# One recurrence block in float32: matrix powers turned by VectorE's 32x32 block transpose instead of by products of transposes, and the grams of two pairs of heads formed beside the powers of two others

## The chip, the cores and the metric

The kernel runs on one core of one Trainium2 chip. The metric is device microseconds of that core. The kernel before took 3894.08 us, the median of three runs (3888.68, 3894.08 and 3894.92 us).

## The reference, cut to what matters

The program is four phases: two transformer layers with different mixers (A and B), a third block with windowed attention (C) and a mixture of experts (D). The change touches only the recurrence in phase B, the RWKV-7 mixer: 16 heads of 64 channels, 512 time steps.

```python
def step(state, inp):
    r_t, w_t, k_t, v_t, a_t, b_t = inp
    sa = jnp.einsum('bhij,bhj->bhi', state, a_t)
    state = (state * w_t[:, :, None, :] + sa[..., None] * b_t[:, :, None, :]
             + v_t[..., None] * k_t[:, :, None, :])
    y_t = jnp.einsum('bhij,bhj->bhi', state, r_t)
    return state, y_t
_, ys = lax.scan(step, state0, seq_inputs)
```

The kernel does it by chunks of 32 steps. With the decays folded into the operands, the steps inside a chunk hang together by a strictly triangular 32x32 matrix N for each head (the masked products of the b and a rows), and the kernel needs the inverse of 1 - N, which is the product (1 + N)(1 + N^2)(1 + N^4)(1 + N^8)(1 + N^16). Four chunks stand on the diagonal of one 128x128 matrix.

## The kernel before, in words

Time is cut into four tiles of 128 steps (`tl` = 0 to 3), heads into eight pairs (`q` = 0 to 7, two heads `u` each). For each tile TensorE does four stages in this order (L2521 to L2545): the *rows* stage turns three operands so that time lies on partitions (24 transposes, each bank of four copied out by ScalarE, L2236); the *pair* stage makes the inverse and what follows from it for all eight pairs; the *chunk* stage runs the state through four chunks one after the other; the *y* stage forms the outputs (L2447, L2451), which VectorE adds to the rest (L2485).

The pair stage goes by groups of two pairs, so there are four groups for each tile and 16 in all. Each engine has its own list of steps (`PAIR_PE`, `PAIR_DVE`, `PAIR_ACT`), and in a group each step is done for one pair and then for the other. Nothing of a group starts before the group ahead has ended: the two pairs of a group fill all four banks of `BK`, and `pp_gram` waits until the last copies of the pairs two before it (`w1_ready`, `w2_ready`) are out. The steps of a pair are:

- *grams*: eight products of 64-row operands (L2286), which VectorE masks out of PSUM (L2355, L2362); ScalarE copies the part that the y stage needs (L2247);
- *low*: the transposed N is had from two more products (L2294), masked by VectorE (L2372), beside 1 + N (L2370);
- *level 1*: N times N (L2313), the transposed square (L2323), and two products with the value rows (L2319, L2321), which VectorE copies out (L2378, L2380);
- *levels 2 to 4*: the next power (L2313, not at level 4), the product of the transposed power with the running inverse (L2315) and the next transposed power (L2323). ScalarE copies both powers out (L2259, L2262) and VectorE adds the product to the running inverse (L2392);
- *last*: the product with the sixteenth power (L2333), added by VectorE;
- *end*: the inverse is put to use in two products for each head (L2343, L2344), copied out by VectorE (L2401) and ScalarE (L2268).

All of it is float32, and one 128x128x128 product appears as two MATMUL records. Where N and its transpose are both wanted, TensorE makes each by a product of its own.

## Time and profile before

| what | us |
|---|---|
| median of three runs | 3894.08 |
| the profiled execution | 3894.22 |
| its span | 3892.4 |
| TensorE matmul busy in the span | 3422.6 (88%) |
| VectorE busy | 1117.3 (29%) |
| ScalarE busy | 1068.5 (27%) |
| mean granted TensorE clock | 0.919 of full |

The recurrence takes the span from about 1122 to 1668 us. A share of busy time says how long an engine had an instruction in flight, not how fast it went; the granted clock is 1.00 at 2.4 GHz and 0.50 at 1.2 GHz. A timeline row gives start, length, engine, line and operation; in square brackets stands how long the engine had been idle and what it had waited for. An instruction's length contains its way through the engine, so that the distance between two starts on a full engine is shorter than the length.

### The profile page before, as it was taken

What the parts mean: (1) busy time and instruction counts of PE and PEld (TensorE: products, weight loads), DVE (VectorE), ACT (ScalarE), POOL (GpSimd) and SP (SyncE); (2) the same over time, 40 slices, a digit from 0 to 9 for tenths busy, and PEclk for the clock granted to TensorE, in tenths of its full rate; (3) what the DMA queues carried; (4) which work ended last, traced back from release to release, by engine and by line L of the source; (5) the groups of instructions that cost most, each with busy time, mean ns of one, the idle gap of its engine ahead of it and who ended that gap; (6) DMA issues with size and microseconds to landing.
All of it is one profiled execution on the core that took longest, in us unless ns stands there. A gap on an engine that the chain in (4) does not pass through costs nothing.

```text
span 3892.4 us, 39687 instructions
## 1 busy us (share of the span) xinstructions
PE 3422.6 (88%) x16652; PEld 2352.5 (60%) x16652; DVE 1117.3 (29%) x1836; ACT 1068.5 (27%) x1818; POOL 709.3 (18%) x344
## 2 busy tenths in 40 slices
PE   7998899979758898888889999988899986989896
PEld 5675688856447777756568876455685562333332
DVE  5342310142763433353231122275131220000001
ACT  3542433334331211213243332134321121111111
POOL 3021344422200000002134441000241121000000
PEclk9999999988877977889999999999999988999998
DMA  3231244311100000022122323210122237989996
GB/s 112 87 108 44 87 162 134 99 58 52 49 0 2 1 1 1 12 87 81 44 82 92 98 87 99 76 33 1 49 77 79 81 119 303 387 327 372 375 375 279
DMA packets 217759, 448.62 MB, mean 115 GB/s; under 512 B 14192, under 2 KB 191376, under 8 KB 204656
## 3 DMA queue, kind: packets, MB, share of 16 engines
q1 hardware_dynamic: 200832, 400.58, 28.4%
q10 hardware_dynamic: 6720, 25.17, 1.6%
q0 software_dynamic: 10032, 20.35, 1.5%
q8 instruction: 133, 2.18, 0.2%
q14 instruction: 42, 0.34, 0.0%
HBM read 502.67 MB, written 31.46 MB: 137 GB/s over the span
## 4 chain that ended last, share of the span: by engine, by line
PE 77%; DMA 8%; DVE 7%; ACT 4%; issue 3%; POOL 1%; SPq 0%; ACTq 0%; POOLq 0%; DVEq 0%
PE product_banks L560 12%; PE product_banks L561 12%; PE product_banks L562 12%; PE product_banks L532 8%; PE product_banks L1859 5%; PE product_banks L1892 3%; DMA A<-in_w_up 3%; DMA Wr<-expert_rows 3%; PE product_banks L624 3%; PE product_banks L2323 2%; PE product_banks L2313 1%; PE product_banks L2315 1%; PE product_banks L1122 1%; PE score_banks L1103 1%; PE product_banks L1339 1%
## 5 line engine op out<-in xcount | busy, mean ns | idle before, releaser
L469 POOL TENSOR_TENSOR Wr_parts<-Wr,Wr_parts 128x1024 fp32r<-128x1024 f32 x186 | 447.2, 2406 | 1429.8 <-ACT Wr_parts L446 1429.8
L561 PE MATMUL product_banks<-A_parts,Wr_parts 128*128 128x512 f32 x1408 | 559.1, 397 | 0.0
L446 ACT ACTIVATE Wr_parts<-Wr 128x1024 fp32r<-128x1024 f32 x186 | 196.0, 1058 | 729.9 <-PE product_banks L562 636.1
L1859 PE MATMUL product_banks<-A,Wr 128*64 128x512 f32 x1504 | 338.9, 598 | 15.7 <-DMA A<-in_w_up 13.3
L560 PE MATMUL product_banks<-H_parts,Wr_parts 128*128 128x512 f32 x728 | 297.2, 408 | 24.4 <-POOL Wr_parts L469 20.8
L561 PEld LDWEIGHTS product_banks<-A_parts,Wr_parts 128*128 128x128 f32 x1408 | 269.6, 191 | 62.0 <-issue 2.2
L560 PE MATMUL product_banks<-A_parts,Wr_parts 128*128 128x512 f32 x680 | 269.8, 397 | 31.1 <-DVE A_parts L482 15.6
L562 PE MATMUL product_banks<-H_parts,Wr_parts 128*128 128x512 f32 x728 | 290.9, 400 | 0.0
L469 POOL TENSOR_TENSOR shared_con_parts<-Wr,shared_con_parts 128x1024 fp32r<-128x1024 f32 x80 | 193.1, 2414 | 446.5 <-ACT shared_con_parts L446 446.5
L562 PE MATMUL product_banks<-A_parts,Wr_parts 128*128 128x512 f32 x680 | 267.8, 394 | 0.0
L1859 PEld LDWEIGHTS product_banks<-A,Wr 128*64 128x64 f32 x1504 | 112.4, 138 | 237.4 <-issue 234.4
L561 PE MATMUL product_banks<-A_parts,shared_con_parts 128*128 128x512 f32 x600 | 239.8, 400 | 0.0
L1892 PE MATMUL product_banks<-A,Wr 128*64 128x512 f32 x752 | 180.9, 627 | 26.7 <-ACT Wr L1928 26.7
L1955 DVE TENSOR_TENSOR Wr<-product_banks,Wr 128x512 f32<-128x512 f32 x24 | 16.6, 692 | 606.9 <-PE product_banks L1859 606.9
L560 PEld LDWEIGHTS product_banks<-H_parts,Wr_parts 128*128 128x128 f32 x728 | 139.4, 192 | 63.5 <-POOL Wr_parts L469 25.8
L560 PEld LDWEIGHTS product_banks<-A_parts,Wr_parts 128*128 128x128 f32 x680 | 129.9, 191 | 63.3 <-POOL Wr_parts L469 18.7
L446 ACT ACTIVATE shared_con_parts<-Wr 128x1024 fp32r<-128x1024 f32 x80 | 84.7, 1059 | 300.5 <-PE product_banks L562 267.4
L2060 DVE SCALAR_TENSOR_TENSOR A<-product_banks,SC 128x512 f32<-128x512 f32 x64 | 44.0, 691 | 415.2 <-PE product_banks L562 415.1
L562 PEld LDWEIGHTS product_banks<-H_parts,Wr_parts 128*128 128x128 f32 x728 | 139.3, 191 | 33.4
L532 PE MATMUL product_banks<-A,Wr 128*128 128x512 f32 (+2 forms) x432 | 148.5, 504 | 0.0
L532 PE MATMUL product_banks<-H,Wr 128*128 128x512 f32 (+1 forms) x384 | 142.1, 531 | 6.5 <-issue 6.5
L562 PEld LDWEIGHTS product_banks<-A_parts,Wr_parts 128*128 128x128 f32 x680 | 129.7, 191 | 27.6
(430 smaller groups left out, 5459.0 us busy)
## 6 DMA issues: line engine op xcount, KB each, us to landing
A<-in_w_gate SPq DMA_DIRECT2D x32, 2048.0 KB
A<-in_w_up SPq DMA_DIRECT2D x32, 2048.0 KB
A<-in_w_down SPq DMA_DIRECT2D x32, 2048.0 KB
Wr<-in_m_w_up SPq DMA_DIRECT2D x32, 1024.0 KB, 5.3
Wr<-in_m_w_down SPq DMA_DIRECT2D x32, 1024.0 KB, 4.9
Wr<-in_w_in SPq DMA_DIRECT2D x32, 1024.0 KB, 5.6
Wr<-in_c_w_kv SPq DMA_DIRECT2D x16, 1024.0 KB, 5.2
expert_rows<-LB ACTq DMA_DIRECT2D x12, 1024.0 KB, 4.2
```

The costliest lines, as they stand in the source:

```text
L446: nc.scalar.activation(weight_parts(s)[0], loaded_part(s), ACT.Copy).then_inc(*mark("weights_high", s))
L469: nc.gpsimd.tensor_tensor(lo, loaded_part(s), hi, ALU.subtract).then_inc(*mark("weights_split", s))
L532: mm = pe.matmul(bank[0:m, 0:width], w[:, k, j * P:j * P + m], rhs(kk), start=(kk == 0), stop=(kk == L.kt - 1))
L560: pe.matmul(bank[:, :], hi[:, k, :], x_hi, start=(kk == 0), stop=False)
L561: pe.matmul(bank[:, :], hi[:, k, :], x_lo, start=False, stop=False)
L562: mm = pe.matmul(bank[:, :], lo[:, k, :], x_hi, start=False, stop=(kk == L.kt - 1))
L624: mm = pe.matmul(bank[:, 0:ww], lhs(k, m), w[:, k, :], start=(k == 0), stop=(k == L.kc - 1))
L1103: mm = pe.matmul(scores[:, q, :], tile(16 + h * dt + d)[:, q * P:(q + 1) * P], key_tile(tag, h * dt + d), start=(d == 0), stop=(d == dt - 1))
L1859: mm = pe.matmul(BK[r, 0 if kind == "gate" else 1, :], XT[b % 2][:, k * P + CAP * h:k * P + CAP * h + CAP], unit_rows((kind, b, h))[:, k, ...
L1892: mm = pe.matmul(BK[r, 2 + n, :], HT[b % 2][:, k * P + CAP * h:k * P + CAP * h + CAP], unit_rows(("down", b, h))[:, k, n * T:(n + 1) * T], ...
L2060: nc.vector.scalar_tensor_tensor(out=tile(40 + j % 4), in0=ps[:, :], scalar=0.0, in1=RS[:, :], op0=ALU.max, op1=ALU.mult).then_inc(*mark(" ...
L2323: mm = pe.matmul(bank[:, 0, 256 + u * P:256 + (u + 1) * P], N, A_, start=True, stop=True)
```

## The change

The transposed powers are no longer made by products. TensorE forms only the next power (`square_pe`) and the product with the running inverse (`inverse_pe`). ScalarE copies the power out, and VectorE turns it with `nc.vector.transpose`, which turns each 32x32 block by itself; as N and its powers are zero outside the 32x32 blocks on the diagonal, that is the whole transpose. The *low* products, their mask and the constant for it are gone.

The banks are shared out anew: `BK` holds only grams; powers and outputs of a pair take half a bank each (`turn_bank` and `stat_bank`); the inverse's products take the `score_banks`, and so does the y stage. Powers, running inverses and turned powers have buffers of their own for two successive groups, and each mask or addition now covers both heads of a pair in one instruction of 128x256 (or 128x512). `lmask` is gone from the constants, the outputs' mask writes its target directly (no copy by ScalarE), and the copies of the value products and of `W2` move from VectorE to ScalarE, whose list follows TensorE's order: powers of level 1, outputs of the two pairs before, value products, powers of levels 2 to 4.

The order of the pair stage is new. The grams of the next two pairs stand behind the first square of the current two, and the *end* of the two pairs before stands behind these. The grams of a tile's first two pairs are formed ahead: for tile 0 before the rows stage, for the others between the chunk stage and the y stage of the tile before. The rows stage moves into a function of its own and is otherwise the same. Lines of the new functions, and of the loops around them:

```diff
@@ -2239,170 +2256,204 @@
+        def square_bank(q):
+            return heads2((B6, B7)[q % 2][:, 0:256])
+        def out_bank(q):
+            return (B6, B7)[q % 2][:, 256:512]
+        def inverse_bank(q):
+            return heads2(S2[:, q % 2, 0:256])
+        def power_act(act, tl, q, level):
+            act.wait_ge(*at("square_done", (tl, q, level)))
+            if level == 1:
+                act.wait_ge(*at("inverse_started", (tl, q)))
+            nc.scalar.activation(power(q), square_bank(q), ACT.Copy).then_inc(
+                *mark("power_ready", (tl, q, level)))
+        def av_act(act, tl, q):
+            act.wait_ge(*at("av_done", (tl, q)))
+            nc.scalar.activation(tile(Y0 + q)[:, tl * P:(tl + 1) * P], out_bank(q)[:, 0:128],
+                                 ACT.Copy)
+            nc.scalar.activation(AV[q % 2], heads2(out_bank(q)[:, 128:256]), ACT.Copy).then_inc(
+                *mark("av_ready", (tl, q)))
+        def pair_out_rows_act(act, tl, q):
             act.wait_ge(*at("pair_done", (tl, q)))
+            nc.scalar.activation(W2[:, :, q, :], heads2(out_bank(q)[:, 0:128]), ACT.Copy)
+            nc.scalar.activation(W1T[:, q, :], out_bank(q)[:, 128:256], ACT.Copy).then_inc(
                 *mark("w1_ready", (tl, q)))
...
+        def gram_pe(pe, tl, q):
             if q >= 2:
-                pe.wait_ge(*at("w2_ready", (tl, q - 2)))
-                pe.wait_ge(*at("w1_ready", (tl, q - 2)))
+                pe.wait_ge(*at("rb_kept", (tl, q - 2)))
             elif tl:
-                pe.wait_ge(*at("wkv_added", (tl - 1, 1)))
+                pe.wait_ge(*at("rb_kept", (tl - 1, q + 6)))
...
+        def square_pe(pe, tl, q, level):
+            pe.wait_ge(*at("power_turned", (tl, q, level - 1)))
+            if level == 2:
+                pe.wait_ge(*at("av_ready", (tl, q)))
             for u in range(2):
+                mm = pe.matmul(square_bank(q)[:, u, :], turned_power(q, level - 1)[:, u, :],
+                               power(q)[:, u, :], start=True, stop=True)
+            mm.then_inc(*mark("square_done", (tl, q, level)))
+        def inverse_pe(pe, tl, q, level):
+            pe.wait_ge(*at("power_turned", (tl, q, level - 1)))
+            if level > 2:
+                pe.wait_ge(*at("inverse_ready", (tl, q, level - 1)))
+            else:
+                pe.wait_ge(*at("inverse_started", (tl, q)))
+                if tl and q < 2:
+                    pe.wait_ge(*at("wkv_added", (tl - 1, 1)))
             for u in range(2):
+                mm = pe.matmul(inverse_bank(q)[:, u, :], turned_power(q, level - 1)[:, u, :],
+                               inverse(q)[:, u, :], start=True, stop=True)
+            mm.then_inc(*mark("inverse_product_done", (tl, q, level)))
+        def av_pe(pe, tl, q):
+            pe.wait_ge(*at("grams_masked", (tl, q)))
+            pe.wait_ge(*at("power_ready", (tl, q, 1)))
+            if q >= 2:
+                pe.wait_ge(*at("w1_ready", (tl, q - 2)))
             for u in range(2):
                 h = 2 * q + u
+                v = VR[:, tl, h * 64:(h + 1) * 64]
+                pe.matmul(out_bank(q)[:, 128 + 64 * u:192 + 64 * u], GM[q % 2][:, u, 0:128], v,
+                          start=True, stop=True)
+                mm = pe.matmul(out_bank(q)[64 * u:64 * u + 64, 0:128], v,
+                               GM[q % 2][:, u, 128:256], start=True, stop=True)
+            mm.then_inc(*mark("av_done", (tl, q)))
+        def pair_end_pe(pe, tl, q):
+            pe.wait_ge(*at("inverse_ready", (tl, q, 5)))
+            if q < 6:
+                pe.wait_ge(*at("power_ready", (tl, q + 2, 1)))
+            for u in range(2):
+                h = 2 * q + u
+                X_ = inverse(q)[:, u, :]
+                pe.matmul(out_bank(q)[:, u * 64:u * 64 + 64], X_, AV[q % 2][:, u, :],
+                          start=True, stop=True)
+                mm = pe.matmul(out_bank(q)[64 * u:64 * u + 64, 128:256],
                                ROW[:, 0, h * 64:(h + 1) * 64], X_, start=True, stop=True)
             mm.then_inc(*mark("pair_done", (tl, q)))
+        def pairs_pe(pe, tl):
+            for q0 in range(0, 8, 2):
+                two = (q0, q0 + 1)
+                for q in two:
+                    square_pe(pe, tl, q, 1)
+                for q in two if q0 < 6 else ():
+                    gram_pe(pe, tl, q + 2)
+                for q in two if q0 else ():
+                    pair_end_pe(pe, tl, q - 2)
+                for q in two:
+                    av_pe(pe, tl, q)
+                for level in (2, 3, 4):
+                    for q in two:
+                        square_pe(pe, tl, q, level)
+                    for q in two:
+                        inverse_pe(pe, tl, q, level)
+                for q in two:
+                    inverse_pe(pe, tl, q, 5)
+            for q in (6, 7):
+                pair_end_pe(pe, tl, q)
+        def strict_dve(dve, tl, q):
             dve.wait_ge(*at("grams_done", (tl, q)))
+            nc.vector.tensor_tensor(power(q), gram_banks(q)[:, :, 0:128], gmask(0), ALU.mult).then_inc(
+                *mark("strict_ready", (tl, q)))
+        def turn_dve(dve, tl, q, level):
+            dve.wait_ge(*(at("power_ready", (tl, q, level)) if level else at("strict_ready", (tl, q))))
+            nc.vector.transpose(turned_power(q, level), power(q)).then_inc(
+                *mark("power_turned", (tl, q, level)))
+        def inverse_start_dve(dve, tl, q):
+            dve.wait_ge(*at("strict_ready", (tl, q)))
+            if q >= 4:
+                dve.wait_ge(*at("pair_done", (tl, q - 4)))
+            nc.vector.tensor_tensor(inverse(q), power(q), ident[:, None, :].broadcast_to([P, 2, P]),
+                                    ALU.add).then_inc(*mark("inverse_started", (tl, q)))
+        def keys_masked_dve(dve, tl, q):
+            dve.wait_ge(*at("grams_done", (tl, q)))
+            if q >= 2:
+                dve.wait_ge(*at("av_done", (tl, q - 2)))
+            nc.vector.tensor_tensor(GM[q % 2], gram_banks(q)[:, :, 256:512], gmask(2, 2),
+                                    ALU.mult).then_inc(*mark("grams_masked", (tl, q)))
+        def outputs_masked_dve(dve, tl, q):
+            if tl and q < 2:
+                dve.wait_ge(*at("wkv_done", (tl - 1, 1)))
+            nc.vector.tensor_tensor(RB[:, 2 * q:2 * q + 2, :], gram_banks(q)[:, :, 128:256], gmask(1),
+                                    ALU.mult).then_inc(*mark("rb_kept", (tl, q)))
+        def inverse_dve(dve, tl, q, level):
+            dve.wait_ge(*at("inverse_product_done", (tl, q, level)))
+            if level == 2:
+                dve.wait_ge(*at("inverse_started", (tl, q)))
+            else:
+                dve.wait_ge(*at("inverse_ready", (tl, q, level - 1)))
+            nc.vector.tensor_tensor(inverse(q), inverse_bank(q), inverse(q), ALU.add).then_inc(
+                *mark("inverse_ready", (tl, q, level)))
+        def pair_begin_dve(dve, tl, two):
+            for q in two:
+                strict_dve(dve, tl, q)
+            for q in two:
+                turn_dve(dve, tl, q, 0)
+            for q in two:
+                inverse_start_dve(dve, tl, q)
+        def pairs_dve(dve, tl):
+            for q0 in range(0, 8, 2):
+                two, ahead = (q0, q0 + 1), q0 < 6
+                for q in two:
+                    turn_dve(dve, tl, q, 1)
+                if ahead:
+                    pair_begin_dve(dve, tl, (q0 + 2, q0 + 3))
+                for level in (2, 3, 4):
+                    for q in two:
+                        turn_dve(dve, tl, q, level)
+                    for q in two:
+                        inverse_dve(dve, tl, q, level)
+                    if ahead and level < 4:
+                        keys_masked_dve(dve, tl, q0 + level)
+                    elif ahead:
+                        outputs_masked_dve(dve, tl, q0 + 2)
+                for q in two:
+                    inverse_dve(dve, tl, q, 5)
+                if ahead:
+                    outputs_masked_dve(dve, tl, q0 + 3)
...
@@ -2438,9 +2489,10 @@
         def y_pe(pe, tl):
 
             pe.wait_ge(*at("rb_kept", (tl, 7)))
-            pe.wait_ge(*at("w2_ready", (tl, 7)))
+            pe.wait_ge(*at("u_ready", 4 * tl + 3))
+
             def out_of(q, u):
-                return BK[64 * u:64 * u + 64, 2 * u + q // 4, (q % 4) * P:(q % 4 + 1) * P]
+                return S2[64 * u:64 * u + 64, q // 4, (q % 4) * P:(q % 4 + 1) * P]
 
             for q in range(8):
                 for u in range(2):
...
+            pe.wait_ge(*at("tilde_ready", 7))
+            for q in (0, 1):
+                gram_pe(pe, 0, q)
             for tl in range(TT):
...
+                rows_pe(pe, tl)
                 pe.wait_ge(*at("rows_ready", (tl, 2, 1)))
-                pe.wait_ge(*at("rows_ready", ("v", TT - 1, 1)))
-                for q0 in range(0, 8, 2):
-                    for f in PAIR_PE:
-                        for q in (q0, q0 + 1):
-                            f(pe, tl, q)
+                pairs_pe(pe, tl)
                 for c in range(4):
                     chunk_pe(pe, tl, c)
                     if tl == TT - 1:
                         norm_sum(pe, "a1_m", 2 * c, 2 * c + 1, width=M)
+                if tl < TT - 1:
+                    for q in (0, 1):
+                        gram_pe(pe, tl + 1, q)
                 y_pe(pe, tl)
             gn_pe(pe)
             product(pe, "w_o", parts(0, 8), low_ready("y"))
...
             nc.vector.memset(ST[:, 0, :, :], 0.0).then_inc(*mark("state_ready", 0))
+            pair_begin_dve(dve, 0, (0, 1))
+            for q in (0, 1):
+                keys_masked_dve(dve, 0, q)
+            for q in (0, 1):
+                outputs_masked_dve(dve, 0, q)
             for tl in range(TT):
-                for q0 in range(0, 8, 2):
-                    for f in PAIR_DVE:
-                        for q in (q0, q0 + 1):
-                            f(dve, tl, q)
+                pairs_dve(dve, tl)
                 for c in range(4):
                     chunk_dve(dve, tl, c)
                 if tl == TT - 1:
                     memory_norm(dve, "a1_")
+                else:
+                    pair_begin_dve(dve, tl + 1, (0, 1))
+                    for q in (0, 1):
+                        keys_masked_dve(dve, tl + 1, q)
                 y_dve(dve, tl)
+                if tl < TT - 1:
+                    for q in (0, 1):
+                        outputs_masked_dve(dve, tl + 1, q)
             gn_dve(dve)
```

## Rows read from the trace of the kernel before

**Rows 1.** The page's busy times and granted clock by slices (whole span).

```profile
PE 3422.6 (88%) x16652; PEld 2352.5 (60%) x16652; DVE 1117.3 (29%) x1836; ACT 1068.5 (27%) x1818; POOL 709.3 (18%) x344
...
PEclk9999999988877977889999999999999988999998
```

**Rows 2.** Pair stages by stretches: us, PE/PEld/DVE/ACT/POOL busy, clock, DMA share, GB/s.

```profile
1127.56:1222.41 94.85, 86.78 (x640) 73.75 (x640) 37.18 (x120) 24.43 (x72) 0.00 (x0) 0.87 0.00 1
1265.04:1354.05 89.01, 80.94 (x642) 69.48 (x644) 37.18 (x120) 24.43 (x72) 0.00 (x0) 0.94 0.00 1
1397.60:1491.10 93.50, 85.40 (x641) 73.11 (x641) 37.18 (x120) 24.43 (x72) 0.00 (x0) 0.89 0.00 1
1533.60:1627.10 93.50, 85.43 (x642) 73.17 (x642) 37.18 (x120) 24.44 (x72) 0.08 (x1) 0.89 0.00 1
```

**Rows 3.** Busy time by stretches: tile 0's y stage, tile 1's rows stage.

```profile
1246.50:1259.40 12.90, 12.90 (x162) 9.78 (x160) 1.38 (x2) 0.00 (x0) 0.00 (x0) 0.50 0.01 3
1259.40:1265.00 5.60, 4.65 (x28) 3.63 (x26) 2.58 (x4) 3.37 (x6) 0.00 (x0) 0.73 0.00 1
```

**Rows 4.** Timeline, start of tile 0's fourth group: grams, masks, low, level 1.

```profile
1201.01 2.06 PE L2286 MATMUL product_banks<-A 64*128 64x128 f32 x32
...
1202.43 0.55 DVE L2362 TENSOR_TENSOR SC<-product_banks,shared_con 128x384 f32<-128x384 f32 x1
1202.89 0.28 DVE L2355 TENSOR_TENSOR Wr<-product_banks,shared_con 128x128 f32<-128x128 f32 x1
...
1205.02 0.49 PE L2294 MATMUL product_banks<-A 64*128 64x128 f32 x4 [0.83 <-DVE SC L2362]
...
1205.82 0.49 PE L2313 MATMUL product_banks<-Wr 128*128 128x128 f32 x2 [0.30 <-DVE Wr L2372]
```

**Rows 5.** Timeline, TensorE in the levels at full clock (third group).

```profile
1192.78 0.39 PE L2323 MATMUL product_banks<-Wr 128*128 128x128 f32 x2
...
1193.00 0.39 PE L2313 MATMUL product_banks<-Wr 128*128 128x128 f32 x2
```

**Rows 6.** Timeline, the end of the fourth group and the first chunk.

```profile
1218.53 0.42 DVE L2392 TENSOR_TENSOR Wr<-product_banks,Wr 128x256 f32<-128x256 f32 x1
...
1218.65 0.68 PE L2333 MATMUL product_banks<-SC 128*128 128x128 f32 x4 [0.16 <-DVE SC L2392]
...
1220.89 0.43 PE L2344 MATMUL product_banks<-SC,A 128*64 128x128 f32 x2
...
1221.62 0.43 PE L2344 MATMUL product_banks<-SC,A 128*64 128x128 f32 x2
...
1222.09 0.28 ACT L2268 ACTIVATE Wr<-product_banks 128x128 f32<-128x128 f32 x1 [1.18 <-PE product_banks L2344]
...
1222.41 1.08 PE L2417 MATMUL score_banks<-Wr 64*32 64x64 f32 x32 [0.37 <-ACT Wr L2268]
```

**Rows 7.** Timeline, TensorE at low clock in the third group.

```profile
1182.82 0.53 PE L2319 MATMUL product_banks<-A,SC 128*128 128x64 f32 x2
...
1184.91 0.53 PE L2319 MATMUL product_banks<-A,SC 128*128 128x64 f32 x2
...
1188.67 0.63 PE L2313 MATMUL product_banks<-Wr 128*128 128x128 f32 x2
...
1189.10 0.63 PE L2315 MATMUL product_banks<-Wr 128*128 128x128 f32 x2
```

**Rows 8.** Busy time by stretches, for the clock (columns as in Rows 2).

```profile
1176.00:1180.00 4.00, 2.52 (x36) 1.94 (x33) 3.31 (x12) 0.83 (x2) 0.00 (x0) 1.00 0.00 0
1180.00:1184.00 4.00, 3.71 (x15) 2.82 (x15) 1.03 (x6) 0.00 (x0) 0.00 (x0) 0.56 0.00 0
...
1488.00:1492.00 4.00, 3.63 (x49) 2.61 (x47) 1.01 (x3) 0.56 (x2) 0.00 (x0) 1.00 0.02 4
```

**Rows 9.** Groups by line and shape, recurrence: ScalarE's copy, VectorE's addition.

```profile
L2259 ACT ACTIVATE SC<-product_banks 128x256 f32<-128x256 f32 x96 | 31.6, 381 | 64.4 <-PE product_banks L2323 64.4
L2392 DVE TENSOR_TENSOR SC<-product_banks,SC 128x256 f32<-128x256 f32 x64 | 27.2, 425 | 47.4 <-PE product_banks L2323 40.6 <-PE product_banks L2333 6.7
```

More of the change, by code:

```diff
@@ L415, in program @@
             last_in[i] = s
-        for name, free in (("w_o", ("start_ready", (TT - 1, 7))), ("cx", ("masked", (NU_ - 1, 2)))):
+        for name, free in (("w_o", ("rb_kept", (TT - 1, 7))), ("cx", ("masked", (NU_ - 1, 2)))):
             if name in split0:
@@ L2238, in rows_act, with gram_banks @@
                         *mark("rows_ready", (tl, n, g)))
[L2242 removed]
+        def gram_banks(q):
             return BK[:, 2 * (q % 2):2 * (q % 2) + 2, :]
[L2245 to L2264 removed]
@@ L2273, in head, with power, inverse, turned_power @@
+        def power(q):
+            return POW[q % 2][q // 2 % 2]
+        def inverse(q):
+            return INV[q % 2][q // 2 % 2]
+        def turned_power(q, level):
+            return TURN[q % 2][(0, 1, 2, 1, 2)[level]]
+        def gmask(part, n=1):
+            return cc("gmask", part * P, n * P)[:, None, :].broadcast_to([P, 2, n * P])
         def head(n, q, u, tl):
             return tile(n + q)[64 * u:64 * u + 64, tl * P:(tl + 1) * P]
-        def pp_gram(pe, tl, q):
+        def power_act(act, tl, q, level):
[4 more added lines that the diff above has]
+                *mark("power_ready", (tl, q, level)))
@@ L2285, in pp_gram @@
                     for u in range(2):
[L2286 removed]
+                        mm = pe.matmul(gram_banks(q)[:, u, (2 * j + i) * P:(2 * j + i + 1) * P],
                                        head(n, q, u, tl), head(r, q, u, tl),
@@ L2548, in rwkv_pe, with rows_pe @@
             branch_sum(pe, "l1o")
+        def rows_pe(pe, tl):
+            for n, src in enumerate((AT_, BT_, KT_)):
+                for g in range(2):
+                    if tl:
+                        pe.wait_ge(*at("state_ready", 4 * tl))
+                    if n:
+                        pe.wait_ge(*at("rows_ready", (tl, n - 1, g)))
+                    elif tl == 0:
+                        pe.wait_ge(*at("rows_ready", ("v", TT - 1, g)))
+                    for i in range(4):
+                        mm = pe.transpose((B6, B7)[g][:, i * P:(i + 1) * P],
+                                          tile(src + 4 * g + i)[:, tl * P:(tl + 1) * P], ident)
+                    mm.then_inc(*mark("turned", (tl, n, g)))
         def turn_pe(pe, src, ready, _, key):
```

184 lines of the change are left out of this document (33 added, 151 removed), and 1 row of the table RINGW.

## The prediction

> **What bounds the kernel now.** I read the page's busy times and clock line first, then the chain of waits and the busy time of each stage, then the timeline of single groups. TensorE is busy for 88% of the span, VectorE for 29% and ScalarE for 27%, and the clock line has its dip in the slices of the recurrence [rows 1]. DMA is near zero in the pair stages [rows 2], so what TensorE saves there nobody else takes. The pair stages last 94.85 + 89.01 + 93.50 + 93.50 = 370.86 us, in which TensorE has a matmul in flight for 338.5 us and VectorE only for 148.7 [rows 2]. The reader is to see three kinds of time in a group of two pairs. In the levels TensorE is full: a 128x128x128 product starts every 0.22 us [rows 5]. Between the grams and level 1 it is nearly empty: the grams (32 records in 2.06 us) start at 1201.01, level 1 at 1205.82, and between them VectorE masks and TensorE waits for it [rows 4]. And the clock falls there: it is 1.00 in the stretch with the gap, where TensorE is busy for 2.52 of 4 us, and 0.56 in the next [rows 8]; level 1 then goes at 2.09 us a head [rows 7]. The fourth group of tile 0, which stays at 1.00, takes 1222.41 - 1201.01 = 21.4 us, against 23.2 us (370.86 / 16) for the mean group.
>
> **Prices.** At full clock: one product 0.22 us, so a level's squares or inverse products for both pairs (four products) 0.89 us [rows 5]; grams of two pairs 1.9 us [rows 4]; end of a head 0.73 us (1221.62 - 1220.89), so 2.9 us for two pairs, and the value products, with the same two shapes, as much [rows 6]. From the first start of two products to their modelled end 0.6 us (0.68 for a waiting set) [rows 6]. ScalarE's 128x256 copy takes 0.38, VectorE's addition 0.42 [rows 9]. VectorE's next instruction starts before the last has ended: a 384-column mask holds it for 0.46 us (1202.43 to 1202.89) [rows 4]; by columns I take 0.33 for 256 and 0.60 for 512. VectorE to TensorE costs 0.16 us, PSUM to ScalarE or VectorE under 0.1 [rows 6]. At 0.50 a product is 0.43 us and a head of level 1 is 2.09, of which two products 0.86, so its value products are 1.23 [rows 7].
>
> The turn of 128x256 has no row. It moves as many columns as the addition and reads one operand instead of two. Lower end: 0.38, a copy's; upper end: twice the addition, 0.85 [rows 9]. I take the addition's 0.42, the nearest row.
>
> The Trainium skill gives a VectorE turn of 128x128 bf16 as 311 ns (VectorE: DVE Perf Modes, The three transpose paths). Its 311 ns against the 0.28 us of the 128-column mask here [rows 4] would make each turn 0.03 us longer, and the sum below, with 6 turns on the path of each of 16 groups, 3 us less of a gain.
>
> **The new group, step by step.** Let T be the start of the last inverse products (`inverse_pe` 5) of a group. TensorE then does these 0.9 us, the next group's first squares 0.9, grams of the pairs after 1.9, ends 2.9, value products 2.9: level 2 starts at T + 9.5. Are the waits covered? The squares read a turn made a whole group before. The grams of the second pair wait for `rb_kept`, a VectorE mask behind the last additions, at about T + 2.2, and are due at T + 2.7. The ends wait for the last additions (T + 1.9) and for the copy of the first square (T + 2.4), both under the grams. VectorE's turn 1, masks, turn 0 and 1 + N of the pairs ahead (eight instructions of 0.33 and three waits) fit into the 7.6 us of grams, ends and value products; queued behind `inverse_start_dve`, which waits for `pair_done` (T + 6.9), is only turn 2, due at T + 10.5. Level 2 of the second pair waits about 0.3 us for ScalarE's two copies.
>
> Levels 2 to 4: TensorE has eight products, 1.8 us. The power's own chain is products 0.6, copy 0.4, turn 0.42, handings-over 0.25, about 1.7 us. VectorE has two turns, two additions and one mask of 512 columns: 4 x 0.33 + 0.6 = 1.9 us. So each level takes about 1.9 to 2.0, VectorE now setting it by a little, and the last inverse product waits for turn and addition of level 4. Walked through in each engine's order it gives 6.5 us from the start of level 2 to the next T. Period: 16.0 us, of which TensorE works 14.8.
>
> A tile: first group without ends 0.9 + 1.9 + 2.9 + 6.5 = 12.2; second and third 16.0 each; fourth without grams and masks 0.9 + 0.9 + 2.9 + 2.9 + 6.0 = 13.6; tail 5.0 (last products and addition about 1.2, two ends 2.9, two copies by ScalarE instead of one and the handing-over 0.9; before, the last head's end to the chunks' start was 0.8 [rows 6]). Together 62.8 us a tile, 251.2 for four.
>
> What is moved and not saved: the first grams of a tile. For tile 0 they stand ahead of the rows stage at full clock, 1.9 us. For tiles 1 to 3 they stand between chunks and y, where the clock is 0.50 [rows 3]: 2 x 1.9 = 3.8 each. Their masks lie under the y stage, 12.9 us in which VectorE has 1.4 us of work [rows 3]. Sum moved: 1.9 + 3 x 3.8 = 13.3. The y stage in two banks instead of four, and the chunks, have the same products; I cost them at nothing (from -3 us for a tile, if the grams let the clock rise ahead of y, to +1).
>
> Gain: 370.86 - 251.2 - 13.3 = 106.4 us. Split by cause: the removed products 12 x 16 x 0.22 = 42 us, the gap between the end of the grams and level 1 16 x 2.9 = 46, the low clock 16 x (23.2 - 21.4) = 29, the waits for last additions and at the joints some 8, less new bubbles of 1.2 us a group, 19. Nothing behind the recurrence has a date of its own: everything starts earlier by as much. From the profiled execution's 3894.2 us (span 3892.4 and 1.8 around it; the median of the runs is 3894.08, the same) comes 3788 us.
>
> **The clock.** This decides most. The falls in the pair stage come behind the gap [rows 4, 8]. At the end of tile 2's last group, where only ends stand for 2.9 us, the clock stays at 1.00 [rows 8]; the new order has ends and value products for 5.8 us in a row, the same shapes with no gap. I take it that it stays.
>
> The Trainium skill warns of short idle spells between groups of matmuls, which by its account make the clock go to and fro although no single wait is long (TensorE: Matmul & The Clock Gate, A second HAM failure mode: psum-queue depth-cycling). That speaks against this change, which puts a wait of some tenths of a microsecond into each level; tile 2's last ends, with TensorE busy for 3.63 of 4 us, keep 1.00 [rows 8].
>
> **Rivals.**
> - *A slow turn.* If it holds VectorE for 0.43 us more (0.85 in all), six turns of each group stand in line between the start of level 2 and T: 6 x 0.43 x 16 = 41 us, time 3829. For it: no row shows a turn. Against: VectorE's instructions go by columns [rows 4, 9]. Chance 0.14.
> - *The clock still falls once in most groups*, in the long run of ends and value products (the level-1 row shows what they cost then). Falls cost a mean group 23.2 - 21.4 = 1.8 us before; if 10 to 16 groups lose 3.5 us, it is 35 to 56: about 3834. Chance 0.15.
> - *Slower than before: the clock stays at 0.50 through the pair stage*, since TensorE, waiting a little in each level, doesn't win it back. Place: every group. Price: 32 products of 0.43, grams 3.8, eight heads of 1.23 = 27.4 us a group, some 438 for the four stages: 3894 + 438 + 13 - 371 = 3974. It decides where a group takes more than (370.86 - 13.3) / 16 = 22.3 us; with 251.2 / 16 = 15.7 at full clock and 27.4 at half, that is low clock for 6.6 / 11.7 = 56% of the work. For it: y and chunk stages stay at 0.50 although TensorE is busy throughout [rows 3]. Against: the levels won the clock back in every group before, for means of 0.87 to 0.94 [rows 2]. Chance 0.05. A turn of over 1.5 us would end on this side too (106.4 / 96 = 1.1 more for each of 96 turns in line): 0.03.
> - *It doesn't do what it says*: the grams ahead wait for masks that come late, and the two pairs run one behind the other. Then each group keeps its 2.9 us gap: 3788 + 46 = 3834. Against: `rb_kept` is due 0.5 us before its use. Chance 0.03.
>
> **How the numbers follow.** Forecast 0.60 (3772 to 3805 by itself: all bubbles gone would give 19 us, turns at 0.6 cost 17). The range 3765 to 3836 takes in the slow turn, the falling clock and the late masks. Slower by over 0.2% (7.8 us, about what a measurement of this kernel tells from no change) is 0.08, the two cases above; within it 0.02, a case between; faster 0.90. Predicted is the likeliest, 3788.
>
> **What would show it.** Right: pair stages of about 63 us with a clock near 1.00; turns of 128x256 near 0.42 us; idle time of TensorE before the last inverse product about 0.4 us, and none before grams, ends and value products; no L2294-like products. Wrong: turns over 0.6 us with TensorE waiting for them in every level; a clock of 0.50 within the value products; y stages that differ from 12.9 us by more than 1 would mean that the moved grams or the two banks matter.

## The result, and the profile after

The changed kernel takes 3779.88 us (median of four runs, 3774.14 to 3785.08) against 3891.38 us before (four runs): the ratio is 0.9712, 95% interval 0.9689 to 0.9735. The profiled execution took 3785.08 us, span 3783.3. The forecast was 3788.

The first two rows are the page's busy times and granted clock by slices; those that follow are busy time by stretches (columns as in Rows 2): the pair stages of tiles 0 and 3, then the y stages of tiles 0 and 3.

```profile
PE 3336.3 (88%) x16140; PEld 2275.6 (60%) x16140; DVE 1130.9 (30%) x1772; ACT 1047.5 (28%) x1786; POOL 710.6 (19%) x344
PEclk9999999988878999788999999989999978999998
```

```profile
1132.00:1196.10 64.10, 61.17 (x480) 51.00 (x480) 36.51 (x94) 19.42 (x64) 0.00 (x0) 1.00 0.01 1
...
1447.70:1511.80 64.10, 61.16 (x480) 50.98 (x480) 36.51 (x94) 19.42 (x64) 0.23 (x1) 1.00 0.00 1
1224.50:1232.10 7.60, 7.60 (x162) 5.93 (x160) 2.94 (x7) 0.00 (x0) 0.00 (x0) 1.00 0.01 2
...
1542.90:1556.00 13.10, 13.07 (x161) 9.80 (x160) 5.01 (x9) 0.47 (x1) 0.00 (x0) 0.50 0.00 1
```

Each of the four pair stages takes 64.1 us, where it took 89 to 95 [rows 2], and its clock is 1.00. The share of busy time hardly moved (88% of the span both times): as a share it says nothing here. The y stage of tiles 0 to 2 takes 7.6 to 8.1 us at a clock of 0.94 to 1.00, where it took 13.0 at half (the stretch in [rows 3] has 12.90 of it); tile 3's is as it was. The forecast had costed the y stages at nothing.

One group in the timeline (start, length, engine, line, operation), from one set of grams (L2315) to the next. L2325 is the next power, L2338 the product with the running inverse, L2397 VectorE's turn, L2426 its addition:

```profile
1146.52 2.06 PE L2315 MATMUL product_banks<-A 64*128 64x128 f32 x32
...
1154.33 0.71 PE L2325 MATMUL turn_bank<-Wr 128*128 128x128 f32 x4
...
1156.43 0.61 PE L2325 MATMUL turn_bank<-Wr 128*128 128x128 f32 x4
...
1158.24 0.71 PE L2325 MATMUL turn_bank<-Wr 128*128 128x128 f32 x4
...
1159.68 0.42 DVE L2397 STREAM_TRANSPOSE Wr<-Wr 128x256 f32<-128x256 f32 x1
...
1160.02 0.40 DVE L2397 STREAM_TRANSPOSE SC<-SC 128x256 f32<-128x256 f32 x1
...
1160.35 0.71 DVE L2426 TENSOR_TENSOR SC<-score_banks,SC 128x256 f32<-128x256 f32 x2
...
1160.88 0.68 PE L2338 MATMUL score_banks<-SC,Wr 128*128 128x128 f32 x4 [0.59 <-DVE SC L2426]
...
1162.83 2.06 PE L2315 MATMUL product_banks<-A 64*128 64x128 f32 x32
```

The period is 16.31 us. The one wait is in front of the last product: VectorE does both turns and then both additions, one behind the other. The mask gap of [rows 4] is gone. What TensorE waited for in all of tile 0's pair stage (us in total, times, longest):

```profile
PE score_banks L2338 <- DVE SC L2426: 2.2, 4, 0.6
PE turn_bank L2325 <- ACT A L2253: 0.7, 1, 0.7
```

**Where the time went, by stages of the traces.** A stage's length is taken from its first matmul to the first matmul of the stage that follows. "Rows and pairs" and "chunks to y" (first chunk product to first y product, with what stands between) are sums over four tiles; "y" (first y product to the next tile's rows stage) is the sum over tiles 0 to 2. The experiments are in it for later.

| kernel | median us | rows and pairs | chunks to y | y |
|---|---|---|---|---|
| before | 3891.4 | 393.1 | 100.7 | 38.9 |
| changed | 3779.9 | 274.9 | 116.8 | 23.7 |
| grams behind | 3793.3 | 288.4 | 112.1 | 28.4 |
| turn twice | 3798.0 | 297.4 | 112.5 | 24.1 |
| products in the new order | 3806.1 | 305.8 | 112.2 | 23.0 |
| grams behind y | 3789.0 | 275.1 | 102.9 | 49.3, grams in it |
| turns, old order | 4011.7 | 499.4 | 107.5 | 38.9 |
| turns, old order, VectorE's queue pair by pair | 3897.1 | 394.8 | 102.0 | 38.9 |
| the same, gap filled | 3836.8 | 333.1 | 103.4 | 38.9 |
| filling between chunks | 3765.6 | 275.1 | 102.8 | 24.0 |

Changed less before: -118.2 + 16.1 - 15.2 = -117.3 us. The first rows stage begins 4.9 us later (2.0 are its grams) and everything behind tile 3's y start takes 3.3 us more, which makes the -109.1 us of the spans. The piece from tile 3's y start on, whose code the experiments don't touch, took 2228 to 2240 us in the traces of all kernels, so some 10 us between two medians may come from there, and the stages are the sharper reading. 5.3 us of it is tile 3's y stage itself, which took 13.03 us at half clock in eight of the fourteen traces (before and changed among them) and 7.70 at full clock in six.

### The profile page after: what moved, and what is told of

It is laid out like the page before. It is cut to its first block, busy times and chain, and to the rows that moved or that the text cites. A ratio compares the mean times of both kernels' runs of the same rounds, so it can differ in the third digit from the quotient of the medians.

```text
span 3783.3 us, 38658 instructions
## 1 busy us (share of the span) xinstructions
PE 3336.3 (88%) x16140; PEld 2275.6 (60%) x16140; DVE 1130.9 (30%) x1772; ACT 1047.5 (28%) x1786; POOL 710.6 (19%) x344
## 4 chain that ended last, share of the span: by engine, by line
PE 77%; DMA 8%; DVE 8%; ACT 4%; issue 3%; POOL 1%; SPq 0%; ACTq 0%; POOLq 0%; DVEq 0%
PE product_banks L560 12%; PE product_banks L561 12%; PE product_banks L562 12%; PE product_banks L532 8%; PE product_banks L1859 5%; PE product_banks L1892 3%; DMA A<-in_w_up 3%; DMA Wr<-expert_rows 3%; PE product_banks L624 3%; PE product_banks L1122 1%; PE score_banks L1103 1%; PE product_banks L1339 1%; PE stat_bank L662 1%; PE product_banks L2315 1%; PE product_banks L583 1%
## 5 line engine op out<-in xcount | busy, mean ns | idle before, releaser
L560 PE MATMUL product_banks<-H_parts,Wr_parts 128*128 128x512 f32 x728 | 298.5, 410 | 24.4 <-POOL Wr_parts L469 20.8
```

The costliest lines, as they stand in the source:

```text
L560: pe.matmul(bank[:, :], hi[:, k, :], x_hi, start=(kk == 0), stop=False)
```

## The experiments

**The gap, in the new order: grams behind the last product.** The order is the changed one, but grams of the next two pairs follow `inverse_pe` 5 of the current ones, and the masks follow them:

```diff
-                for q in two if q0 < 6 else ():
-                    gram_pe(pe, tl, q + 2)
...
                 for q in two:
                     inverse_pe(pe, tl, q, 5)
+                for q in two if q0 < 6 else ():
+                    gram_pe(pe, tl, q + 2)
```

> The changed kernel with one thing undone: the grams of the next two pairs stand behind a group's last inverse products instead of beside its level 1, so that TensorE waits for mask and turn at each of the 12 joints inside tiles. Theory (ends and value products cover the masks, the clock stays): a wait of about 1.2 us at each joint, less some 0.4 us a group for levels freed of the masks, 8 to 12 us in all, about 3790 us, pair stages 64.1 -> 66 to 67 us with the clock at 1.00. Rival (the gap itself makes the clock fall, as in the kernel before): the stages' mean clock comes back to 0.87 to 0.94 and they lose 8 to 10 us each, about 3815.

3793.29 us, ratio to before 0.9761 (0.9733 to 0.9789). Rows and pairs take 13.5 us more; the pair stages 3.2 us each, so 1.1 us at each of the 12 joints between two groups. Two of TensorE's waits in tile 0's pair stage:

```profile
PE turn_bank L2325 <- DVE Wr L2397: 2.6, 3, 0.9
PE score_banks L2338 <- DVE SC L2426: 1.8, 4, 0.5
```

The clock of all four pair stages is still 1.00. So waits of 0.9 us don't bring it down. The gap of 2.9 us ahead of level 1 [rows 4] is mostly covered here already, by ends and value products. Tile 1's y stage, though, took 13.0 us at half clock again, with the same 3.7 us of grams ahead of it:

```profile
1332.80:1345.80 13.00, 13.00 (x162) 9.80 (x160) 2.94 (x7) 0.00 (x0) 0.00 (x0) 0.50 0.01 3
```

**What a turn costs: each done twice.** The first one goes into spare columns that nobody reads:

```diff
+            spare = 1024 + 256 * (len(turns) % 4)
+            nc.vector.transpose(heads2(shared[:, spare:spare + 256]), power(q))
```

> The changed kernel with every turn done twice (first into a spare buffer that nobody reads). Theory of the prediction (six turns of each group stand in line between level 2 and the last inverse product): each turn holds VectorE for 0.33 to 0.36 us more, 96 x 0.35 = 34 us, about 3814. Rival (VectorE is idle for most of the time and hides it): under 8 us, about 3785.

3798.03 us, ratio 0.9765 (0.9741 to 0.979). Rows and pairs take 22.5 us more for 96 turns that I had put in line (6 in each of 16 groups): 0.23 us each, not the 0.34 that a turn holds VectorE (1159.68 to 1160.02). About a third is hidden. The wait in front of the last product grew to 1.4 us at the longest, and the clock of the pair stages stayed at 1.00:

```profile
PE score_banks L2338 <- DVE SC L2433: 4.9, 4, 1.4
```

**The removed products: turned powers by products again, in the new order.** Twelve more products of 128x128x128 in each group; VectorE turns only N itself:

```diff
+                mm = pe.matmul(heads2(out_bank(q))[:, u, :], power(q)[:, u, :],
+                               turned_power(q, level - 1)[:, u, :], start=True, stop=True)
...
-                    for q in two:
-                        turn_dve(dve, tl, q, level)
```

> The changed kernel with its new order, but the turned powers of levels 1 to 4 made by products of transposes again (12 more products for a group of two pairs, copied out by ScalarE; only the first matrix is still turned by VectorE). Theory (TensorE's work sets the stage): 12 x 0.22 x 16 = 42 us more, less up to 12 us of bubbles that go, 3810 to 3822. Rival (the chain from square to copy to turn sets it, which is shorter by a turn here): under 10 us, or a gain, 3775 to 3790.

3806.05 us, ratio 0.9793 (0.9768 to 0.9818). Rows and pairs take 30.9 us more for 12 x 16 x 0.22 = 42 us of products, since they fill the waits as well. The new order with all that comes with it (the *low* products gone, wider masks, copies by ScalarE) is thus worth some 82 us (before took 3887.8 us beside it), and the turned powers add 26 to it (31 by the stages).

**The y stage: grams behind it instead of ahead**, and their masks with them.

```diff
+                y_pe(pe, tl)
                 if tl < TT - 1:
                     for q in (0, 1):
                         gram_pe(pe, tl + 1, q)
-                y_pe(pe, tl)
```

> The changed kernel with the first grams of tiles 1 to 3 behind the y stage of the tile before instead of ahead of it. Theory (the dense grams win back the clock, and so the y stage that follows runs at 1.00): the y stages of tiles 0 to 2 go back from 7.6 to 12.9 us at 0.50, 3 x 5.3 = 16 us more, of which the grams, next to dense transposes, may give back up to 5: 3791 to 3796. Rival (the y stage is faster for its two banks or other neighbours): the y stages stay near 7.6 us, about 3780.

3788.96 us, ratio 0.9749 (0.9722 to 0.9777). The y stage is back at half clock, 12.90 us:

```profile
1220.90:1233.80 12.90, 12.90 (x162) 9.80 (x160) 1.38 (x2) 0.00 (x0) 0.00 (x0) 0.50 0.01 3
```

From first rows to tile 3's y it is 11.9 us more than in the changed kernel. In the changed kernel (timeline) the grams run at low clock ahead of y, and y's first products are at full clock (0.44 us for four records, 0.70 in tile 3):

```profile
1220.88 3.70 PE L2315 MATMUL product_banks<-A 64*128 64x128 f32 x32
1224.51 0.44 PE L2499 MATMUL score_banks<-Wr,A 128*64 128x128 f32 x4
```

The same grams, 3.6 to 3.8 us of them, and the same two banks stand in both kernels; only the place of the grams differs. Ahead of y they win the clock back, though not each time: over all traces 19 of the 21 y stages with grams right ahead of them went at full or nearly full clock (0.91 to 1.00), and none of the 21 of tiles 0 to 2 without. The two misses are tile 1's with the grams behind the last product (above) and tile 0's in the last variant below.

Tile 3's y, where no grams of a next tile stand, went at full clock here although nothing ahead of it was changed:

```profile
1554.90:1562.50 7.60, 7.60 (x161) 5.87 (x160) 5.42 (x10) 0.47 (x1) 0.00 (x0) 1.00 0.01 2
```

It did so in three of the eleven traces in which no unread products stand behind tile 3's last chunk, so this stage finds either level with the same instructions right ahead of it; what decides it, no run here shows. It gave this kernel back 5.3 us of what its other y stages lost.

**The turns alone, in the old order.** TensorE's low and transposed products go, VectorE turns, all else stands:

```diff
-        PAIR_DVE = [pd_mask, pd_low, pd_av, pd_level(2), pd_level(3), pd_level(4), pd_level(5),
+        PAIR_DVE = [pd_mask, pd_low, pd_av, pd_turn(1), pd_turn(2), pd_level(2), pd_turn(3),
+                    pd_level(3), pd_turn(4), pd_level(4), pd_level(5),
```

> The kernel before in its old order of work (two pairs at a time, grams, masks, then levels), with one part of the change alone: the transposed powers are turned by VectorE, and the products of transposes are gone from TensorE (12 products of 128x128x128 fewer a group). Theory: in this order each level is bound by its chain, product, ScalarE's copy, VectorE's turn, next product, so TensorE has less to do but waits instead, and the gap with the masks ahead of level 1 stays. A level cost 2.65 us of products before (twelve of 0.22) and should cost about 2.2 now; with the low product's 0.8 us gone too a group falls from 21.4 to some 18.5 to 20 us at full clock, while the clock still falls behind the gap: 3894 less 16 x 1.5 to 2 = about 3865, between 3840 and 3880. Rival: the products removed are what counts and the order little: 16 x 5 = 80 us or more of the gain are here already, 3810 or less.

4011.65 us, ratio 1.0307 (1.0285 to 1.0328): both theories wrong. Timeline of two successive levels:

```profile
1180.35 0.45 DVE L2370 STREAM_TRANSPOSE SC<-SC 128x256 f32<-128x256 f32 x1 [0.45 <-ACT SC L2256]
1180.72 0.39 DVE L2390 TENSOR_TENSOR Wr<-product_banks,Wr 128x256 f32<-128x256 f32 x1
...
1181.25 0.46 PE L2306 MATMUL product_banks<-Wr 128*128 128x128 f32 x2 [1.35 <-DVE Wr L2390]
...
1184.62 0.68 PE L2324 MATMUL product_banks<-Wr 128*128 128x128 f32 x4 [1.35 <-DVE Wr L2390]
```

A level takes 3.38 us, not 2.2. Each step of `PAIR_DVE` is done for both pairs, so the first pair's addition (L2390) stands behind the second pair's turn, which stands behind ScalarE's copy, which stands behind the second pair's products: the two pairs no longer cover each other.

**The same with VectorE's queue in another order**: addition and turn of one pair, then of the other.

```diff
+        PAIR_DVE = [pd_mask, pd_low, both(pd_av, pd_turn(1)), both(pd_level(2), pd_turn(2)),
+                    both(pd_level(3), pd_turn(3)), both(pd_level(4), pd_turn(4)), pd_level(5),
```

> The old order with turns on VectorE again, which took 4011 us, but VectorE now does a pair's addition and then its turn before it goes to the second pair; in the kernel that took 4011 us it did both turns of a level first, then both additions, so the first pair's addition stood behind the second pair's turn and TensorE waited 1.35 us for it in each level (a level every 3.38 us). Theory: this order of VectorE's queue is most of what was lost. A level should take 2.1 to 2.2 us (products of a pair 1.2, copy 0.38, turn 0.42, handing over), 1.2 us less in three levels and 0.9 in front of the last product: some 4.5 us in each of 16 groups, 72 us, so about 3940, between 3910 and 3960. What is left over the kernel before would then be the clock, which is at 0.50 for longer because the waits between levels let it come back late. Rival: the chain of product, copy and turn itself is the price whatever the queue's order: less than 1 us a group, 3995 or more. A second rival: with the waits short the clock holds and the products removed show, 3865 or less.

3897.13 us, ratio 1.0019 (1.0009 to 1.0029). The queue's order was 115 us of the loss (72 were expected). But with 12 products a group fewer on TensorE, the *low* products gone and the longest wait in the levels down to 0.5 us, the kernel is no faster than before. Tile 0's wait ahead of level 1, and tile 1's pair stage by stretch:

```profile
PE product_banks L2306 <- DVE Wr L2363: 10.8, 4, 2.7
...
1264.90:1359.20 94.30, 80.86 (x518) 66.62 (x520) 49.75 (x144) 18.94 (x50) 0.00 (x0) 0.80 0.00 1
```

The clock is 0.80, where it was 0.87 to 0.94 [rows 2]: half clock for 40% of the time, 9.4 us of a group, so 4.7 us lost in each of 16 groups, 75 in all. In the kernel before, the same sum over the pair stages (length times what the clock lacks to 1.00) is 38 us. So what the products gave (42 us) went to the clock.

The gap doesn't bring the clock down each time. Here it fell in all 16 groups; in the kernel before, where 2.75 us lie between grams and level 1 in every group (the *low* products in it), it fell in 8 of 16, and a group with a fall took 23.9 to 26.1 us, one without 21.0 to 21.4. Two stretches of tile 1 there, the gap and level 1 behind it, with no fall (compare [rows 8]):

```profile
1288.00:1292.00 4.00, 2.24 (x18) 1.55 (x17) 3.56 (x14) 0.83 (x2) 0.00 (x0) 1.00 0.02 4
1292.00:1296.00 4.00, 4.00 (x30) 3.28 (x30) 0.67 (x3) 0.84 (x3) 0.00 (x0) 1.00 0.00 0
```

**The same with the gap filled.** Twelve products that nobody reads, between grams and level 1, where TensorE waits 2.7 us for the masks:

```diff
+                    if q % 2 == 0:
+                        for i in range(12):
+                            pe.matmul(B7[:, 0:P], ident, ident, start=True, stop=True)
```

> The old order with turns (addition and turn pair by pair, 3897 us) with 12 products of 128x128x128 that nobody reads in the gap between a group's grams and its level 1, where TensorE waits 2.7 us for VectorE's masks (12 x 0.22 = 2.65 us at full clock, so level 1 isn't late by more than 0.1 us). In the kernel without them the clock of the pair stages is 0.80, a group takes 23.4 us, and the low clock begins with level 1, right behind the gap. Theory: the gap is what brings the clock down. Filled, it stays at 1.00, and a group takes what it works at full clock, about 18.4 us: 16 x 5 = 80 us less, about 3817. Rival: the value products and ends, small tiles, bring it down as well, gap or not: then a group gains under 1 us and the time is 3885 or more. Between the two: the clock falls in part of the groups, as it did in the kernel before.

3836.79 us, ratio 0.9877 (0.9853 to 0.9901). The four pair stages take 77.5 us each, first gram to first chunk product, at a clock of 1.00. By stretches, one group:

```profile
1147.69:1166.96 19.27, 18.96 (x153) 16.19 (x152) 12.43 (x36) 4.46 (x12) 0.00 (x0) 1.00 0.01 2
```

More work, 60 us less time. So the gap does bring the clock down in this order, and dense work in it holds the clock through value products and ends. A group takes 19.27 us, 0.9 more than the 18.4 I had worked out. The changed kernel's 16.31 is 2.96 us below, with the same products but for the unread ones, which take 2.78 us of the group (grams' end to level 1): that is the gap, in which the changed kernel does the next pairs' grams and the ends of the pairs before.

**A further version: filling between chunks.** In the changed kernel TensorE waits 1.57 us between two chunks, and a chunk takes 5.1 us at full clock (tile 0's first) and 7.1 at half (those behind it), from one start of L2468 to the next:

```profile
1196.14 1.08 PE L2468 MATMUL score_banks<-Wr 64*32 64x64 f32 x32 [0.54 <-ACT Wr L2304]
...
1201.25 1.92 PE L2468 MATMUL score_banks<-Wr 64*32 64x64 f32 x32 [1.57 <-issue]
...
1208.34 0.96 PE L2468 MATMUL score_banks<-Wr 64*32 64x64 f32 x14 [1.57 <-issue]
```

`fill_pe(pe, 7)` is seven products of 128x128x128 that nobody reads, 84 in all.

```diff
                     if tl == TT - 1:
                         norm_sum(pe, "a1_m", 2 * c, 2 * c + 1, width=M)
+                    if c < 3:
+                        fill_pe(pe, 7)
```

> The changed kernel with seven products of 128x128x128 whose result nobody reads, put where TensorE waits 1.57 us between two chunks (behind chunks 0 to 2 of every tile, 84 products in all). A chunk takes 5.1 us while the clock is 1.00 (tile 0: 1196.14 to 1201.25) and 7.1 us at 0.50 (1201.25 to 1208.34). Theory: the clock falls because of that wait, and dense work in its place keeps it at 1.00: the stretch from the chunks to y takes about 22.7 us instead of 28.4 in tiles 0 to 2, some 17 us in all, and tile 3 gains some 5: about 3760 to 3765. Rival: the clock falls anyway, from the chunks' small tiles themselves; then the added products at 0.43 us cost 7 x 0.43 - 1.57 = 1.4 us for each of 12 waits: 17 us more, about 3797.

3765.58 us (3764.44 to 3765.94), ratio 0.968 (0.9661 to 0.9698): with one variant below, the fastest kernel here, 14 us below the changed one. The intervals of the two ratios overlap; chunks to y take 14.0 us less in all, which is the surer reading. The theory came within 1 us of the time and was wrong on the way: chunks to y take 27.0, 24.1 and 23.6 us in tiles 0 to 2, not 22.7. Tile 1, two stretches of the chunk stage:

```profile
1303.00:1308.00 5.00, 5.00 (x55) 4.61 (x56) 1.24 (x3) 0.00 (x0) 0.00 (x0) 0.51 0.01 3
1308.00:1313.00 5.00, 4.95 (x115) 4.53 (x113) 2.37 (x4) 0.00 (x0) 0.00 (x0) 1.00 0.00 0
```

The clock still falls, so the wait isn't its only cause; the dense products win it back after a chunk, and in this tile it then holds to the end of y. In tile 0 it falls and comes back four times, the last time with the grams ahead of y.

**Variants of it.** First grams between the chunks (behind chunks 1 and 2), three unread products with each:

> The same filling, but part of it is work that has to be done anyway: the first grams of tiles 1 to 3 stand behind chunks 1 and 2 of the tile ahead (with three idle products each), not in a row behind chunk 3; behind chunk 0, and behind all three chunks of tile 3, seven products that nobody reads. Theory: grams are dense enough to hold the clock as the products do; the grams' time behind chunk 3 (1.9 us at full clock, 3.7 at half) goes from each of three tiles: 5 to 6 us less than the kernel with the plain filling if that one holds the clock, about 3757. Rival: without grams ahead of y the clock falls in the y stage again (13 us instead of 8): 15 us more than the kernel with the plain filling.

3770.84 us, ratio 0.9692 (0.9672 to 0.9713). The rival's way, not its price of 15 us: chunks to y take 6.3 us less than with the plain filling, but y is at half clock again (12.2 to 12.6 us in tiles 0 to 2), and the rows stages behind it take 3.7 us more. Tile 3's y went at full clock:

```profile
1537.40:1545.00 7.60, 7.60 (x161) 5.88 (x160) 5.44 (x10) 0.47 (x1) 0.00 (x0) 1.00 0.01 2
```

Then 14 unread products behind tile 3's last chunk as well:

> As the kernel before it in this set, with 14 more products that nobody reads behind tile 3's last chunk, ahead of its y stage, where no grams of a next tile stand. Theory: they take 3.1 us at full clock (6.0 at half) and y then takes 7.6 to 8 us instead of 13.1, if the clock was at half there: a gain of 0 to 2 us; if the clock was held at 1.00 by the filling between chunks they are a plain cost of 3.1 us. Rival: tile 3's y stays at 13.1 us all the same, and the cost is 3 to 6 us.

3776.95 us, ratio 0.9707 (0.9688 to 0.9726). The median rose by 6 us. The trace without the 14 products had tile 3's y at full clock already, 7.70 us in both, so here they bought nothing and cost 3.2 us: the plain cost that the theory had for a clock already at 1.00. What is left of the rise lies behind tile 3's y, in code that is the same; it stays open. With the plain filling:

> The kernel with seven unread products between two chunks, and 14 more behind tile 3's last chunk, where no grams of a next tile stand. Theory: ahead of tile 3's y stage dense work wins the clock back as it did in the kernel where this was tried with the grams between the chunks (8 heads of y from 1539.5 to 1547.2, not 13.0 us); the products cost 3.1 to 3.3 us, y gains 5.3: 2 us less than without, about 3763. Rival: the clock is 1.00 ahead of them already or they come at 0.50 throughout: 1 us more or nothing.

3765.55 us, ratio 0.9681 (0.9663 to 0.9698): no difference. The products cost 4.3 us (they begin at half clock) and y gained 5.3, since without them it was at half clock. Last, four products between chunks, not seven, with the 14 kept:

> As the kernel just named, with four unread products between two chunks and not seven (0.88 us at full clock, well within the wait of 1.57 us). Theory: what the filling does is to win the clock back after it has fallen in a chunk, and fewer products do that less often: the stretch from chunks to y lies between 24.9 (mean of tiles 0 to 2 with seven) and 28.5 us (with none), so some 3 to 8 us more in all, 3766 to 3771. Rival: the wait's mere length counts, which four products shorten nearly as well while they never make a chunk late: 2 to 4 us less than with seven, about 3760.

3774.7 us, ratio 0.9699 (0.9681 to 0.9716): 9 us more than with seven, and beyond the 3766 to 3771 expected. Chunks to y take 26.2 to 27.6 us in tiles 0 to 2, and tile 0's y fell to half clock in spite of the grams ahead of it. The intervals of the two ratios overlap; the stages of the two traces differ by 10 us. So it is dense work winning the clock back that counts, more than the shorter wait.

## Why the prediction was right, step by step

**Right: the period.** From the start of level 2 to the last product 6.55 us (forecast 6.5); from there to the next level 2 9.76 (forecast 9.5, the parts rounded down: 0.97 + 0.98 + 1.99 + 2.90 + 2.92). A tile takes 64.1 us and not 62.8, so the pair stages gained 5 us less than forecast. Ends, grams and value products wait for nothing, as said.

**Right: the turn at an addition's price.** The trace has the turns at 436 and 423 ns (80 each) and the additions at 402. The 311 ns of the Trainium skill (VectorE: DVE Perf Modes, The three transpose paths) is for a bf16 128x128 turn, which no run here shows; its premium of 0.03 us is about what the trace has. The rival of a slow turn had a place, but too high a price: by the doubled turns 0.43 us more would have cost 0.23 / 0.34 of 41 us, some 28 by this estimate. The rival of the late masks was priced too high as well: with the grams put behind the last products the stages took 13.5 us more, not 46.

**Right: the clock stays up.** 1.00 through all pair stages, even with waits of up to 1.4 us in the groups (turn twice). The warning of the Trainium skill about short idle spells between groups of matmuls (TensorE: Matmul & The Clock Gate, A second HAM failure mode: psum-queue depth-cycling) didn't come true here at 0.6 to 1.4 us. The 2.7 us gap ahead of level 1 is the cause of the falls in the old order with turns, shown by filling it. For the kernel before it is taken over from there: its falls come behind the same gap, but in 8 of 16 groups only, which the forecast didn't look at. One reading under the third rival doesn't hold: [rows 3] shows a y stage busy throughout at 0.50, but no chunk stage, and tile 0's chunk stage had TensorE busy for 19.15 of 24.4 us at a clock of 0.63.

**Right in sum, off in the split.** I split the gain into removed products 42, gap 46, low clock 29. Parts don't add like that: in the old order the turns alone gave nothing, since the clock took what they freed; in the new order they give 26 to 31 us. The low clock is worth up to 60 us where the turns are in already; in the kernel before it took 33 us by the lengths of its groups (21.0 us at full clock for the first three of a tile, 21.4 for the last), not 29. The gap's 46 agrees with 16 x 2.96 = 47. But placing the grams ahead gives only 13.5 of it; the rest comes from ends and value products standing where TensorE waited.

**Wrong: the y stage.** Costed at nothing, it gave 15.2 us. The prediction named it as its lower bound (-3 us a tile if the grams let the clock rise), but the price of that bound was wrong: a whole y stage at full clock is 5 us less, not 3. The moved grams themselves were sized right (2.0 + 3.6 + 3.7 + 3.7 = 13.0 against 13.3). None of the rest was costed either: the rows stages gained 3.9 us (3.5 of them behind the faster y stages), the chunks lost 5.0, the first rows stage began 2.9 later than its grams explain and what follows tile 3's y start took 3.3 more. These and the 5.3 us of the pair stages cancelled to within 3 us, so that the forecast is 3 us off the spans and 8 off the median partly by luck.

## What to carry to other kernels

Before a product is taken off TensorE, ask what fills its place: an engine that is only relieved waits, and here a wait of 2.7 us in front of small tiles cost about as much in clock as the products had. Work that has to be done anyway and is dense (here the grams) was worth 4 us a tile more right ahead of a stage of small tiles than behind it (11.9 us over three tiles). Where two streams are interleaved to cover each other, write each engine's queue stream by stream: turn, turn, add, add in place of add, turn, add, turn cost 115 us here.

## What the runs showed of the hardware that I had not expected

TensorE busy in all of a stretch can stay at half clock when its tiles are small (y stage, 12.90 us busy of 12.90, clock 0.50), and 3.6 to 3.7 us of grams just ahead took the same stage to 7.60 us at 1.00, in 19 of 21 cases. Tile 3's y stage shows how little decides it: with the same instructions right ahead it took 7.70 us in three traces and 13.03 in eight. A gap of 2.75 us was followed by a fall of the clock in 8 of 16 groups of one kernel and by none in the others. Adding 192 products that nobody reads made one kernel 60 us faster (3897 to 3837), and adding 84 another 14 (3780 to 3766). With the grams spread between the chunks, a few microseconds earlier, the y stages of tiles 0 to 2 fell back to half clock.
